# Which engine sums the adaptive chunks, and where their loads stand: one edit of a two-block transformer kernel

## What is computed

```python
cond = jax.nn.silu(c)
for i in range(2):
    shift, scale, gate = jnp.split(cond @ ada_w[i] + ada_b[i], 3, axis=-1)
    h = rms_norm(x, norm_g[i]) * (1 + scale[:, None, :]) + shift[:, None, :]
    y = nsa_mixer(h, ...) if i == 0 else moba_mixer(h, ...)
    x = x + gate[:, None, :] * y
```

## Time and profile before

| | |
|---|---|
| median of 3 runs | 969.85 us (969.57 to 970.19) |
| profiled execution | 970.32 us, its span 968.5 us |
| mean granted clock of TensorE | 0.979 |
| busy: TensorE, VectorE, ScalarE, GpSimd | 94%, 59%, 50%, 18% |
| DMA | 163.26 MB, 169 GB/s over the span |

### The profile page before, as it was taken

How to read it: one execution, slowest core, us unless ns; L and a number is a source line. 1 busy time by engine, 2 the same in 40 slices (tenths; PEclk the granted TensorE clock), 3 DMA queues, 4 the chain that set the end, 5 groups by cost and what they waited for, 6 DMA issues and landing times.

```text
span 968.5 us, 13044 instructions
## 1 busy us (share of the span) xinstructions
PE 905.7 (94%) x5021; PEld 778.5 (80%) x5021; DVE 573.8 (59%) x917; ACT 484.2 (50%) x756; POOL 175.6 (18%) x192
## 2 busy tenths in 40 slices
PE   2779898999889999999999999999999899999998
PEld 2568897899778988888888888888789788888886
DVE  4884577444866637755555446767356665555543
ACT  2143574455544645654545447586663555444431
POOL 1006335255206441000000001452001100000000
PEclk9889998999989999999999999999999999999999
DMA  9855646155646255555555565553234556555650
GB/s 344 312 162 179 204 143 232 44 153 149 197 135 198 78 161 180 165 183 187 178 195 195 175 178 185 162 154 110 68 107 143 163 180 199 185 175 180 210 175 22
DMA packets 45693, 163.26 MB, mean 169 GB/s; under 512 B 5185, under 2 KB 5441, under 8 KB 45633
## 3 DMA queue, kind: packets, MB, share of 16 engines
q1 hardware_dynamic: 45632, 162.44, 52.6%
HBM read 161.37 MB, written 1.05 MB: 168 GB/s over the span
## 4 chain that ended last, share of the span: by engine, by line
PE 85%; DVE 8%; ACT 3%; issue 1%; DMA 1%; POOL 1%; SPq 0%; DVEq 0%; ACTq 0%
PE bank L481 56%; PE bank L490 11%; PE bank L505 4%; DVE w_lo L1517 2%; PE bank L645 2%; PE bank L534 1%; DVE mx L1670 1%; PE bank L651 1%; DVE ada_acc L1617 1%; DMA w_raw<-in_weights 1%; PE bank L728 1%; PE bank L671 1%; PE bank L673 1%; PE bank L672 1%; ACT kh L1038 1%
## 5 line engine op out<-in xcount | busy, mean ns | idle before, releaser
L1034 ACT ACTIVATE w_hi<-w_raw 128x1024 fp32r<-128x1024 f32 (+2 forms) x249 | 258.9, 1046 | 194.4 <-PE bank L481 161.0
L1517 DVE TENSOR_TENSOR w_lo<-w_raw,w_hi 128x1024 fp32r<-128x1024 f32 (+2 forms) x249 | 304.6, 1241 | 81.9 <-ACT w_hi L1034 81.3
L481 PE MATMUL bank<-w_hi,h_hi 128*128 128x512 f32 (+1 forms) x576 | 229.3, 398 | 16.3 <-DVE w_lo L1517 8.2
L481 PE MATMUL bank<-w_hi,h_lo 128*128 128x512 f32 (+1 forms) x576 | 225.6, 392 | 0.0
L481 PE MATMUL bank<-w_lo,h_hi 128*128 128x512 f32 (+1 forms) x576 | 225.1, 391 | 0.0
L481 PEld LDWEIGHTS bank<-w_hi,h_hi 128*128 128x128 f32 x576 | 109.5, 190 | 38.9 <-issue 17.9
L481 PEld LDWEIGHTS bank<-w_hi,h_lo 128*128 128x128 f32 x576 | 109.2, 190 | 22.9
L481 PEld LDWEIGHTS bank<-w_lo,h_hi 128*128 128x128 f32 x576 | 109.4, 190 | 21.1
L2277 POOL TENSOR_TENSOR ada_acc<-ada_acc,w_raw 128x512 f32<-128x512 f32 x56 | 78.2, 1396 | 101.6 <-ACT w_raw L1038 96.3
L490 PE MATMUL bank<-h_hi,w_hi 128*128 128x256 f32 x264 | 79.6, 302 | 3.7 <-DVE tokq L1599 3.0
L490 PE MATMUL bank<-h_hi,w_lo 128*128 128x256 f32 x264 | 77.1, 292 | 0.0
(11 more groups left out here) (297 smaller groups left out, 1351.0 us busy)
## 6 DMA issues: line engine op xcount, KB each, us to landing
w_raw<-in_weights SPq DMA_DIRECT2D x298, 512.0 KB, 3.8
w_raw<-in_weights SPq DMA_DIRECT2D x4, 360.0 KB, 4.4
x<-in_x SPq DMA_DIRECT2D x1, 1024.0 KB, 6.5
gate_row<-in_gate_bias SPq DMA_DIRECT2D x2, 512.0 KB, 10.1
out<-x SPq DMA_DIRECT2D x4, 256.0 KB, 3.2
w_raw<-in_weights SPq DMA_DIRECT2D x3, 256.0 KB, 2.7
const<-in_constants SPq DMA_DIRECT2D x1, 413.5 KB, 7.1
cols<-in_columns SPq DMA_DIRECT2D x1, 208.5 KB, 2.5
```

The costliest lines, as they stand in the source:

```text
L481: mm = e.matmul(pb[t][:, 0:n], xs[q], ws[p], start=(k + kk == 0 and i == 0), stop=(k + kk == kts - 1 and i == 2))
L1034: e.activation(w_hi[i % NSPLIT][:, 0:c], raw[v % NRAW][:, 0:c], ACT.Copy).then_inc(*rounded(v))
L1517: e.tensor_tensor(w_lo[i % NSPLIT][:, 0:c], raw[v % NRAW][:, 0:c], w_hi[i % NSPLIT][:, 0:c].bitcast(F32), ALU.subtract).then_inc(*rested(v))
```

## The change

Chunks 4 and 5 are summed by VectorE (`mac_chunk`) instead of ScalarE and GpSimd. Their eight units move in the order of loads from among z to among `nsa_q0`, `cmp_w1_0`, `nsa_q1` and `cmp_w1_1`, one behind every two units; VectorE takes them at the second and fourth unit of each, and its look-ahead there is 3. TensorE's `ada_columns` 4 and 5 move to the first and third unit of `nsa_vsvw`, into bank 7. The units of chunk 6 come among z, one behind every two, and those of chunks 7 to 9 are spread over the eight attention steps by `SLOT_UNITS`; their columns are taken at steps 2, 4, 6 and 8 instead of 4, 6, 8 and 10.

```diff
--- before.py
+++ after.py
@@ -31,6 +31,8 @@
 EPS = 1e-6
 NEG, FLOOR = -1e30, -1e29
 UNIT = 1024
+ON_VECTOR = range(6)
+SLOT_UNITS = ((4, 5), (6,), (7, 8), (9,), (10, 11), (12,), (13, 14), (15,))
 Z_FIRST = 5
 NRAW, NSPLIT = 7, 4
 HALVES = (slice(0, 64), slice(64, 128))
@@ -65,10 +67,12 @@
     one = lambda name, k=KT, n=512, split=True: units_of([(name, k, n, split)])
     two = lambda name, k=KT: one(f"{name}0", k) + one(f"{name}1", k)
     z, out, out2 = two("moba_z"), two("nsa_out"), two("moba_out")
-    a, b = ada(0, 4, 6) + ada(1, 0, 4), ada(1, 4, 6)
+    gate, a, b = ada(0, 4, 6), ada(1, 0, 4), ada(1, 4, 6)
     heads = one("nsa_q0") + one("cmp_w1_0", CJ, 256, False) + one("nsa_q1") + one("cmp_w1_1", CJ, 256, False)
-    nsa = (in_turn(one("nsa_z0") + one("nsa_z1"), a[:8]) + a[8:14] + out[0:1] + a[14:18] + out[1:2] + a[18:22]
-           + out[2:3] + a[22:] + out[4:6] + out[3:4] + out[6:])
+    heads = [u for i in range(8) for u in heads[2 * i:2 * i + 2] + gate[i:i + 1]]
+    z01 = one("nsa_z0") + one("nsa_z1")
+    nsa = ([u for i in range(4) for u in z01[2 * i:2 * i + 2] + a[i:i + 1]] + a[4:9] + out[0:1] + a[9:12] + out[1:2]
+           + a[12:15] + out[2:3] + a[15:] + out[4:6] + out[3:4] + out[6:])
     moba = in_turn(b[:3], z[Z_FIRST:]) + b[3:] + out2[0:3] + out2[4:5] + out2[3:4] + out2[5:]
     early, kcvc, kskw = ada(0, 1, 2) + ada(0, 3, 4), one("nsa_kcvc"), one("nsa_kskw")
     order = (ada(0, 0, 1) + ada(0, 2, 3)
@@ -509,7 +513,7 @@
 
                 acc, n = ada_acc[(c // 2 if c < 4 else c) % 2], c % 6
                 w.wait_ge(*const_in.at())
-                w.wait_ge(*(ada_mac if c < 4 else ada_summed).at((c, KT - 1)))
+                w.wait_ge(*(ada_mac if c in ON_VECTOR else ada_summed).at((c, KT - 1)))
                 w.wait_ge(*free)
                 if n < 4:
                     for j in range(4):
@@ -775,6 +779,7 @@
             for j in linear("nsa_vsvw", 1, (h_hi, h_lo), h_of(0), True, [gelu_done.at((1, 1))]):
                 if j == 0:
                     compress_down(1, banks[6], heads_placed.at(("nsa_kskw", 1)))
+                    ada_columns(4, banks[7], modulated.at((0, 3)))
                 if j == 1:
                     w.wait_ge(*gate_tanh.at())
                     w.wait_ge(*heads_placed.at(("nsa_kskw", 0)))
@@ -783,7 +788,8 @@
                     q_turns("nsa_q0", 0, banks[5], kc_placed.at())
                 if j == 2:
                     q_turns("nsa_q0", 1, banks[4], gates_done.at())
-            first = {0: modulated.at((0, 3)), 1: v_done.at(("nsa", 1)), 2: v_done.at(("nsa", 1)),
+                    ada_columns(5, banks[7], gate_row_done.at(4))
+            first = {0: gate_row_done.at(5), 1: v_done.at(("nsa", 1)), 2: v_done.at(("nsa", 1)),
                      3: heads_placed.at(("nsa_q0", 1))}
             for j in linear("nsa_z0", 0, (h_hi, h_lo), h_of(0), False, [gate_biased.at()]):
                 if j == 0:
@@ -798,8 +804,6 @@
                 if j < 2:
                     compressed_scores(j, (banks[5], banks[6]),
                                       (c_masked.at(0) if j else heads_placed.at(("nsa_q1", 1)),))
-                if j == 2:
-                    ada_columns(4, banks[0], z_done.at(("nsa_z0", 1)))
                 if j == 3:
                     compressed_turns(0, banks[1], z_done.at(("nsa_z0", 1)))
 
@@ -810,19 +814,17 @@
 
             def nsa_hook(i):
                 if i == 0:
-                    compressed_turns(1, banks[0], gate_row_done.at(4))
-                if i == 1:
-                    ada_columns(5, banks[0], pc_done.at(1))
+                    compressed_turns(1, banks[0], z_done.at(("nsa_z0", 1)))
                 if i in (4, 6, 8):
                     next(outs[0])
-                if i in (4, 6, 8, 10):
-                    ada_columns(4 + i // 2, banks[0], o_gated.at(("nsa", i // 2 - 2)))
+                if i in (2, 4, 6, 8):
+                    ada_columns(5 + i // 2, banks[0], o_gated.at(("nsa", i // 2 - 2)) if i > 2 else pc_done.at(1))
                 if i in (9, 10):
                     next(outs[1])
 
             pair_attention("nsa", [v_done.at(("nsa", 1)), pc_done.at(1), zeroed.at(3)],
                            [[m_reduced.at(("nsa", 23)), c_masked.at(1)], [m_reduced.at(("nsa", 23)), pc_done.at(0)],
-                            lambda pr: ada_cols.at(5 + pr) if pr else gate_row_done.at(5)], nsa_hook)
+                            lambda pr: ada_cols.at(6 + pr)], nsa_hook)
             next(outs[0])
             next(outs[1])
             next(outs[1])
@@ -1116,7 +1118,7 @@
                     k = units[u][1] + kk
                     src = raw[u % NRAW][:, kk * 512:(kk + 1) * 512]
                     if k == 0:
-                        w.wait_ge(*ada_turned.at(c - 2 if c > 5 else (1, 3)[c - 4]))
+                        w.wait_ge(*ada_turned.at(c - 2))
                     copy(ada_acc[c % 2][:, :] if k == 0 else src, src,
                          scale=cond[:, k:k + 1]).then_inc(*ada_scaled((c, k)))
 
@@ -1274,7 +1276,8 @@
                     q_places("nsa_q1", "nsa_q", 0, banks[6])
                 if j == 2:
                     q_places("nsa_q1", "nsa_q", 1, banks[5])
-                scale_chunk(4, j)
+                if j % 2:
+                    scale_chunk(6, j // 2)
 
             def compressed_weights(tt):
                 w.wait_ge(*c_shifted.at(tt))
@@ -1294,7 +1297,8 @@
                 if j == 0:
                     z_half("nsa_z0", 0, 0)
                     z_half("nsa_z0", 0, 1)
-                scale_chunk(5, j)
+                if j % 2:
+                    scale_chunk(6, 2 + j // 2)
                 if j == 2:
                     compressed_weights(0)
                 if j == 3:
@@ -1307,7 +1311,7 @@
                     z_half("nsa_z1", 1, 0)
                     z_half("nsa_z1", 1, 1)
                 if step == 1 and i < 8:
-                    for k in (2 * i, 2 * i + 1):
+                    for k in SLOT_UNITS[i]:
                         scale_chunk(6 + k // 4, k % 4)
                 if step == 1 and i in (2, 4, 6):
                     rounds(of["nsa_out0"][i // 2 - 1], 0)
@@ -1607,10 +1611,10 @@
                     w.wait_ge(*cond_done.at())
                     for kk in range(units[u][2]):
                         k = units[u][1] + kk
-                        acc, src = ada_acc[c // 2 % 2][:, :], raw[u % NRAW][:, kk * 512:(kk + 1) * 512]
+                        acc, src = ada_acc[(c // 2 if c < 4 else c) % 2][:, :], raw[u % NRAW][:, kk * 512:(kk + 1) * 512]
                         if k == 0:
-                            if c in (1, 3):
-                                w.wait_ge(*ada_turned.at(c - 1))
+                            if c not in (0, 2):
+                                w.wait_ge(*ada_turned.at({1: 0, 3: 2, 4: 1, 5: 3}[c]))
                             e.tensor_scalar(acc, src, cond[:, k:k + 1], None, ALU.mult).then_inc(*ada_mac((c, k)))
                         else:
                             w.wait_ge(*ada_mac.at((c, k - 1)))
@@ -1869,26 +1873,34 @@
                                         bcast(col(f"pe{i}").unsqueeze(2).unsqueeze(3), [P, CJ, NKV, NCMP]),
                                         ALU.add).then_inc(*flat_done(i))
             for j, u in enumerate(of["nsa_q0"]):
-                rests(u)
+                rests(u, 3)
+                if j % 2:
+                    mac_chunk(4, j // 2)
                 if j == 0:
                     head_sums("nsa_kskw")
                 if j == 2:
                     head_scales("nsa_kskw")
             for j, u in enumerate(of["cmp_w1_0"]):
-                rests(u)
+                rests(u, 3)
+                if j % 2:
+                    mac_chunk(4, 2 + j // 2)
                 if j == 0:
                     head_sums("nsa_q0")
                 if j == 3:
                     head_scales("nsa_q0")
             for j, u in enumerate(of["nsa_q1"]):
-                rests(u)
+                rests(u, 3)
+                if j % 2:
+                    mac_chunk(5, j // 2)
                 if j == 2:
                     w.wait_ge(*kc_power.at())
                     w.wait_ge(*rows_in.at())
                     e.scalar_tensor_tensor(kc2[:, 0, :], banks[5][:, 0:HD], kc_rs, row("nsa_kc"), ALU.mult,
                                            ALU.mult).then_inc(*kc_normed())
             for j, u in enumerate(of["cmp_w1_1"]):
-                rests(u)
+                rests(u, 3)
+                if j % 2:
+                    mac_chunk(5, 2 + j // 2)
                 if j == 0:
                     k_rests("nsa_kskw", "nsa_ks", 0, banks[4])
                     k_rests("nsa_kskw", "nsa_kw", 1, banks[6])
@@ -1904,10 +1916,12 @@
             w.wait_ge(*kc_rounded.at())
             e.tensor_tensor(kc_hl[:, 1, :], banks[5][:, 0:P], kc_hl[:, 0, :].bitcast(F32),
                             ALU.subtract).then_inc(*kc_placed())
+            ada_column(4, banks[7])
```

(13 more changed lines are left out.)

## The result

The changed kernel takes **973.8 us** (median of 6 runs, 972.87 to 974.69) where the kernel before took 969.71 beside it (6 runs, 969.46 to 970.63): a ratio of 1.004, interval 1.0029 to 1.005. That is 3.8 us above the predicted 970.0, inside the range of 966 to 975 but outside the likeliest case of 968 to 972. It is slower by over 0.2%, to which the prediction gave 0.34, against 0.38 for a change within 0.2%. The profiled execution took 972.87, with a span of 971.1.

The account below looks back on a forecast made before the run. TensorE, busy 94% of the span, was taken as the bound, so other engines count only where it waits or its clock falls. Terms summed to +0.15 us on the median of 969.85, giving 970.0; range 966.0 to 975.0.

Parts of the forecast that it names:

- `nsa_q1` held: Late load, splits and multiply-adds delay the scales of `nsa_q0`, so TensorE starts `nsa_q1` late: +3.7 us.
- wait before the gate: Key scales come later before the gate projection, TensorE idle 4.5 instead of 3.05 us: +1.45.
- idle of the z stage: From `nsa_z0` to the attention, TensorE idle 4.4 instead of 5.9 us: -1.5.
- clock of the z stage: The half-clock stretch between `nsa_z0` and the attention disappears, as remaining waits are below 1.75 us: -4.9.
- attention's tail: At the attention's end, GpSimd's last sum is out before the `w_lo` at 249.11, which no longer stretches: -1.0 us.
- Stage 1: `nsa_q0` to `cmp_w1_1`, which receives 8 units: VectorE's multiply-adds cost by their places, not their total of 12.8 us.
- The chain of the ring: A load issues only when the unit seven places earlier is released; `nsa_q1`'s second unit therefore lands at 87.4.
- (a): The new waits before `nsa_q1` and the gate cost no clock (two terms of 2.4 gone): 967.6 us; chance 0.20.
- (b): `nsa_q1` isn't held, because its load or the scales come earlier than placed: 962.4 us; chance 0.06.
- rival (c): Clock falls again in `nsa_z`, behind the wait before group 14: slower, 971.7 to 974.9 us; chance 0.24.
- Exclusion against the powers: VectorE's multiply-adds and `w_lo` wait out GpSimd's powers: 1.0 us before `nsa_q1`, 3 to 4 before the gate; chance 0.03.
- rival (d): `nsa_z0` and `nsa_z1` yield nothing, or VectorE waits out GpSimd's powers: 974 to 976.4 us; chance 0.10.

Follow-up runs that it names:

- thin z sums: GpSimd's sums of chunk 6 made over 8 of 512 columns, on the changed kernel: 974.31 us; on the reordered one: 965.83 us.
- later splits: VectorE's splits in `nsa_z0` drawn three units ahead instead of four, on the changed kernel: 973.8 us; on the reordered one: 964.88 us.
- The two experiments without a fall there: Changed kernel with thin z sums (974.31 us) and with later splits (973.8 us).
- reordered: Changed kernel with new load order, multiply-adds where VectorE was idle, `nsa_q1`'s scales ahead of its splits and other look-aheads up to the gate: 964.79 us.

## Why the prediction was right and wrong

By its own steps, in the profiled executions (measured: the first table, after against before; the two gate-row products at 0.87 each, half of 22.28 - 20.54, which is taken as saved in their old places too):

| step | predicted | measured |
|---|---|---|
| `nsa_q1` held | +3.7 | +4.0 |
| clock behind it | +1.6 | +1.7 |
| wait before the gate | +1.45 | +1.1 |
| longer fall behind the gate | +0.8 | +0.9 |
| gate-row products moved | 0 | 0 (+1.74 - 1.74) |
| idle of the z stage | -1.5 | -1.4 (5.88 to 4.52) |
| clock of the z stage | -4.9 | -2.5 |
| attention's tail | -1.0 | -0.7 |
| sum | +0.15 | +3.1 |

- **Stage 1 was right in mechanism and size**: 7.55 predicted, 7.7 found, 8.0 by the medians. The chain of the ring, the order on VectorE and even the times hold (`nsa_q1` at 93.99 for 92.95, with the whole trace 0.7 later there; gate wait 4.15 for 4.5, as the power was out at 117.15 and the scales started 1.0 behind it). In the first half the scales of `nsa_kskw` came later than forecast: they ended at 82.59, 0.15 us ahead of TensorE instead of 0.8, as the short GpSimd instruction between sums and power took 1.49 us beside a `w_lo` (last section). TensorE lost nothing by it. `nsa_q1`'s first unit was late too, which the prediction doesn't say: it lies seven behind a gate unit, which VectorE released at 84.0. Rivals (a) and (b) are refuted by the windows at clock 0.91 and 0.50 and by the 3.93.
- **The z stage is where it failed**: 45.05 us where 42.5 was forecast, 2.5 of the 3.0 us that the sum misses in these traces. In the prediction's terms it is the clock: "Both waits left are below 1.75, so I let the fall go", booked at -4.9. The waits were indeed below 1.75 (0.76 and 1.67 before groups 9 and 11), and a fall came behind the 1.67. An idle time from one place was taken as a bound that holds in another. What happened is rival (c), to which 0.24 was given, with the fall one unit earlier than it said.
- **The stage's two parts say more than the term does.** Behind group 14 the clock was full after, as forecast. There the fall of before was worth 4.45 us and not 4.9: group 17 to attention took 17.98 before and 12.66 after, 0.87 of the difference being the gate-row product. The forecast took half of the busy time at half clock as lost; the matmuls there ran at more than half speed (last section). The rest of the miss lies up to group 14, which the prediction had about 0.7 longer (-0.4 before group 11, +1.1 before group 14) and which was 2.6 longer (22.33 for 19.73). With thin z sums it was 0.9 longer. So the larger part, 1.7 us, is what the prediction said would be gone: splits stretched by chunk 6's sums (1.5 us of VectorE's time); the rest of the 1.7 may be the fall's. Up to group 14 a fall of 3.4 us hardly costs, by the pair with the later splits.
- **The place of the waits was wrong too, though their sum was right** (-1.4 for -1.5). The 1.35 before group 11 was to be free of stretched splits; the pair at 149.62 was stretched by 1.1 us beside the sums of chunk 6. The 1.5 before group 14 was 0.43 while TensorE was at half clock ahead of it. The two experiments without a fall there show 1.28 and 2.40.
- **Attention's tail**: the wait for `w_lo` shrank from 1.79 to 0.70, the predicted 1.0; a wait of 0.62 for `parts_of_o` at 196.48, where before has only one of 0.23 (at 198.31), took 0.4 of it back.
- **Exclusion against the powers** (in rival (d)) did not occur. That the time, 973.8, is near the 974 forecast for it is chance. After, the power ran from 86.09 to 89.46 and from 113.78 to 117.15; the `w_lo` pairs at 88.72 and 114.27 took 2.48 and 2.37, as undisturbed ones do, and the two multiply-adds at 85.14 the usual 1.53.
- **The range held by its rivals**: without what was kept in it for (c) and half of (d) it would have ended at 972, and the time lies above that.

Between the profile's +3.1 and the medians' +4.1 lies 1 us that these traces do not place. Outside the six stretches the after trace is 0.7 longer up to `cmp_w1_0` and 1.3 shorter behind the second norm, in parts where single half-clock stretches are 3.4 us longer in one trace than in the other; and the profiled execution was the fastest of its six. Longer falls in the z stage, as two of the experiments show, would give it, but that was not seen in this kernel.

## What to carry to other kernels

Work put onto an engine with idle time costs by its place in that engine's order more than by its amount: the same 16 multiply-adds and 8 loads cost 8 us in one order and nothing in another, and making the multiply-adds nearly free in the first order took back less than half. What mattered was which load lies one ring length behind a late release, and what stands ahead of the instruction that the critical engine waits for. Before a moved unit is placed, walk its ring predecessors and put the awaited scaling first. In a stretch where another engine sets the pace, don't book the end of a clock fall as a gain, nor tune single waits: the idle and the slow clock trade with each other until that engine has less to do. Behind such a stretch a fall costs in full, and an edit that is right by itself can lose its gain to a fall that moves there.

## What the runs showed of the hardware

- The length of an idle time does not decide alone whether the clock falls behind it: 1.75 us was followed by full clock before, 1.67 by half clock after and by full clock with the thin z sums. With the later splits one and the same wait, before group 11, was followed by full clock once (2.01 us, changed kernel) and by half clock once (2.02, reordered). What decides was not settled.
- A fall can cost nothing: with the later splits the part paced by VectorE took 21.97 us without one and 21.96 with one of 3.4 us. Behind that part one of 3.4 us cost 1.5.
- At half clock these matmuls were not half as fast: those of 256 columns, one behind another, started 0.213 us apart at half clock and 0.12 at full (the changed kernel, 159.5 to 162.5 and from 162.7), 1.8 times as far.
- Small GpSimd instructions are stretched beside VectorE's, the other way round from what the prediction weighed. An instruction over 128x16 values took 1.49 us beside a `w_lo` and the multiply behind it (75.94 to 77.56 on VectorE), 0.26 before; one over 128x32 values took 1.23 beside the pair at 88.72 and ends with it:

```profile
76.12 1.49 POOL L2259 TENSOR_SCALAR stats<-stats 128x16 f32<-128x16 f32 x1 [57.87 <-DVE stats L1583]
...
86.09 3.37 POOL L2262 TENSOR_TENSOR stats<-stats 128x16 f32<-128x16 f32 x1
...
90.08 1.23 POOL L2249 TENSOR_TENSOR rope_tmp<-tokk,nsa_ks_sin 128x32 f32<-128x32 f32 x1
```

The Trainium skill (SBUF — State Buffer, SBUF: two separate sides, and Who interferes with whom) has the two engines exclude each other for a whole instruction when VectorE has two SBUF inputs and GpSimd reads SBUF. These short instructions agree with it. The power of 3.37 us, which also reads SBUF, does not: the two `w_lo` from 114.27 to 116.64 started and ended inside one that ran from 113.78 to 117.15, at their usual length.
